# Gate projections with the tokens as the moving operand, key sums as rows, two more held input units and a fused state decay in a two-layer hybrid decoder step

## The reference

```python
def trunk(x, ...):
    for l in range(2):
        h = rmsnorm(x, gl[0])
        mix = even_mixer(h, ...) if l == 0 else odd_mixer(h, ...)
        x = x + rmsnorm(mix, gl[1])
        h = rmsnorm(x, gl[2])
        x = x + rmsnorm(squared_relu_mlp(h, w_ff1[l], w_ff2[l]), gl[3])   # 1024 -> 4096 -> 1024

def even_mixer(h, S0, ...):       # layer 0: gated DeltaNet (4 heads, 128x128 state) beside a gating MLP
    qkv, gate, beta_pre, a_pre, u_pre, v_pre = split_cols(h @ w_in, ...)  # beta_pre, a_pre: 4 columns each
    ...
    S = S * gl_c[..., None, None] + einsum('bhik,bhiv->bhkv', kd_c, v_new)

def odd_mixer(h, C0, n0, m0, ...):  # layer 1: mLSTM (4 heads, 128x256 state C, 128-element key sum n)
    q, k, v, i_pre, f_pre, o_pre = split_cols(h @ w_in, ...)              # i_pre, f_pre: 4 columns each
    ...
    Cm = keep[..., None, None] * Cm + einsum('bhj,bhjd,bhjv->bhdv', wk, k_c, v_c)
    n = keep[..., None] * n + einsum('bhj,bhjd->bhd', wk, k_c)
```

## Time and profile before

| | |
|---|---|
| median of 3 executions | 2915.94 us (2915.1 to 2921.61) |
| the profiled execution, its own time | 2918.17 us |
| span of its instructions | 2916.4 us |
| PE busy | 2785.1 us, 95% of the span |
| DVE busy, ACT busy | 1390.2 us, 1171.1 us |
| mean granted clock of TensorE | 0.961 |

### The profile page before, as it was taken

One profiled execution on the slowest core, in us unless ns is written; L12 is line 12 of the kernel. 1 busy time (PEld: TensorE's weight loads), 2 busy tenths in 40 slices (PEclk: granted clock), 3 DMA queues, 4 the chain that ended last, 5 costly groups with the idle time before them and its releaser, 6 DMA issues.

```text
span 2916.4 us, 41138 instructions
## 1 busy us (share of the span) xinstructions
PE 2785.1 (95%) x17217; PEld 2482.0 (85%) x17217; DVE 1390.2 (48%) x2130; ACT 1171.1 (40%) x2024; POOL 209.9 (7%) x343
## 2 busy tenths in 40 slices
PE   7889999799999999999999999999999899999997
PEld 5779988688888769889999998998776687999997
DVE  4545554645554446443444446434444337444344
ACT  6454445455554335333333335333332235333323
POOL 5011100100000000110000001110000000000000
PEclk9899999999999999899999999999999899999998
DMA  5343222522323224543332325543245634343222
GB/s 179 118 130 103 85 67 87 161 62 90 91 74 91 80 87 146 166 141 95 102 95 75 114 73 160 157 136 98 87 136 95 98 90 148 98 127 114 87 88 71
DMA packets 365928, 313.61 MB, mean 108 GB/s; under 512 B 11217, under 2 KB 338923, under 8 KB 365744
## 3 DMA queue, kind: packets, MB, share of 16 engines
q1 hardware_dynamic: 336224, 207.91, 25.8%
q0 software_dynamic: 29520, 103.07, 11.0%
HBM read 256.02 MB, written 54.91 MB: 107 GB/s over the span
## 4 chain that ended last, share of the span: by engine, by line
PE 73%; issue 10%; DVE 6%; ACT 6%; DMA 3%; POOL 1%; ACTq 0%; POOLq 0%; DVEq 0%
PE dense L519 60%; PE mixer L519 11%; DMA wst<-in_w_ff_dram 2%; ACT whi L993 2%; DVE wlo L1467 2%; ACT arena L993 1%; DVE hf L1610 1%; DMA xl<-xd 1%; PE mixer L735 1%; ACT ffh L993 1%; ACT L993 1%; DVE hlo L1606 0%; DVE ffh L1506 0%; ACT relu L993 0%; DVE accA L1543 0%
## 5 line engine op out<-in xcount | busy, mean ns | idle before, releaser
L519 PE MATMUL dense<-hhi,whi 128*128 128x272 f32 (+1 forms) x3072 | 865.0, 336 | 32.0 <-DVE hlo L1606 12.1
L519 PE MATMUL dense<-hhi,wlo 128*128 128x272 f32 (+1 forms) x3072 | 836.4, 327 | 0.0
L519 PE MATMUL dense<-hlo,whi 128*128 128x272 f32 (+1 forms) x3072 | 835.3, 326 | 0.0
L1467 DVE TENSOR_TENSOR wlo<-wst,whi 128x1024 fp32r<-128x1024 f32 x384 | 470.6, 1226 | 371.8 <-ACT whi L993 371.6
L519 PEld LDWEIGHTS dense<-hhi,whi 128*128 128x128 f32 x3072 | 524.4, 192 | 95.7 <-issue 32.2
L993 ACT ACTIVATE whi<-wst 128x1024 fp32r<-128x1024 f32 x384 | 404.2, 1053 | 449.8 <-PE dense L519 410.6
L519 PEld LDWEIGHTS dense<-hhi,wlo 128*128 128x128 f32 x3072 | 522.3, 192 | 43.8
L519 PEld LDWEIGHTS dense<-hlo,whi 128*128 128x128 f32 x3072 | 525.0, 192 | 38.1 <-issue 1.0
L519 PE MATMUL dense<-h1hi,whi 128*128 128x272 f32 (+1 forms) x1536 | 431.3, 335 | 18.3 <-DVE wlo L1467 11.0
L519 PE MATMUL dense<-h1lo,whi 128*128 128x272 f32 (+1 forms) x1536 | 420.8, 328 | 0.0
L519 PE MATMUL dense<-h1hi,wlo 128*128 128x272 f32 (+1 forms) x1536 | 419.1, 327 | 0.0
(11 more groups left out here) (304 smaller groups left out, 2015.8 us busy)
## 6 DMA issues: line engine op xcount, KB each, us to landing
wst<-in_w_ff_dram SPq DMA_DIRECT2D x256, 512.0 KB, 3.9
wst<-in_w_in_even_dram SPq DMA_DIRECT2D x48, 512.0 KB, 3.8
wst<-in_w_in_odd_dram SPq DMA_DIRECT2D x48, 512.0 KB, 3.8
proj<-ffh POOLq DMA_DIRECT2D x48, 272.0 KB, 2.4
proj<-ffh POOLq DMA_DIRECT2D x48, 256.0 KB, 2.3
arena<-proj POOLq DMA_DIRECT2D x8, 1536.0 KB, 9.6
wst<-in_w_out_even_dram SPq DMA_DIRECT2D x16, 512.0 KB, 3.6
xl<-xd POOLq DMA_DIRECT2D x32, 256.0 KB, 3.1
```

The source lines that it names most:

```text
L519: return pe.matmul(out, lhsT, rhs, start=start, stop=stop)
L1467: TT(wlo[:, u % 2, :], wst[:, u % 2, :], whi[:, u % 2, :].bitcast(F32), ALU.subtract)\
```

## The change

1. **Gates.** The 16 (and 8) gate columns become the stationary operand and the tokens the moving one: for each of 8 blocks of channels two products, of one matmul of 512 columns in group 0 and two of 272 in group 1. ACT copies the 16 rows into `relu2`; one dense unit later a new item `gate2` turns them to token rows and adds the two halves, with small float32 matmuls against the identity, two for each tile; DVE copies them out. The split of `wg` is an item of its own (`wgs`), four units ahead of the gate.
2. **Held units.** `SEQ_2` holds 6 units (14 and 15 added), `SEQ_1` has 18 in another order. The loads of norm 2's residual use four buffers, two of them in `relu2`.
3. **Decay.** In `gdn_sample` the multiplication and the two additions become 8 fused operations of 128x128.
4. **Key sums.** n of all samples and heads is loaded as 32 rows of 512 bytes by one DMA, turned by one PE transpose and copied into `CS` by DVE; new values are gathered by DVE, turned back at the end together with the prompt's, and stored by two DMAs. PE waits for the copies (`ms_nset`).

```diff
-SEQ_1 = [0, 20, 1, 21, 2, 22, 3, 23, 4, 5, 12, 6, 7, 13, 8, 9, 14, 10, 11, 15]
-SEQ_2 = [16, 17, 18, 19]
+SEQ_1 = [0, 20, 1, 2, 21, 3, 4, 22, 5, 6, 23, 7, 8, 12, 9, 10, 11, 13]
+SEQ_2 = [14, 15, 16, 17, 18, 19]
...
+            if gate is not None and g == 0 and i == gate - 4:
+                rows[-1].append(("wgs", l))
             if i == gate:
                 rows[-1].append(("gate", l, g))
+            if gate is not None and i == gate + 1:
+                rows[-1].append(("gate2", l, g))
...
+            if r == 0:
+                return (xl if c % 4 < 2 else relu2)[:, c % 2, :], ("xl", "xr")[c % 4 // 2] + str(c % 2), c // 4 + 1
...
             def gate(l, g):
-                for i, t in enumerate(range(*GT[g])):
-                    _, c, n = tok(t)
-                    for k in range(KT):
-                        mm(DB[0:n, b, i * 16:(i + 1) * 16], hhi[g][:, k, c], wg2[:, k, :], start=k == 0, stop=False)
-                        last = mm(DB[0:n, b, i * 16:i * 16 + 8], hlo[g][:, k, c], wg_hi[:, k, :],
-                                  start=False, stop=k == KT - 1)
+                for k in range(KT):
+                    for rows, w, x in ((16, wg2[:, k, :], hhi[g]), (8, wg_hi[:, k, :], hlo[g])):
+                        for q, (c0, c1) in enumerate(PARTS[g]):
+                            last = mm(DB[0:rows, b + q, 0:512] if g == 0 else DB[0:rows, b + q, 0:272], w,
+                                      x[:, k, 272 * q:272 * (q + 1)] if g else x[:, k, 0:512],
+                                      start=k == 0 and rows == 16, stop=k == KT - 1 and rows == 8)
+                last.then_inc(S("job_done"), 1)
+
+            def gate_turn(l, g):
+                evac_wait(pe, ("gate", l, g))
+                for i, t in enumerate(range(*GT[g])):
+                    _, c, n = tok(t)
+                    for half in range(2):
+                        last = mm(DB[0:n, b, i * 8:(i + 1) * 8], relu2[0:16, 0, c],
+                                  ident[0:16, 8 * half:8 * half + 8], start=half == 0, stop=half == 1)
...
-                    link(TT(ss, ss, bcl(gls[:, :].rearrange("p (b h) -> p b h", h=H)[:, :, h], [P, NB, P]), ALU.mult))
                     dve.wait_ge(S("gs_ds"), h + 1)
-                    for q in range(2):
-                        last = TT(ss[:, 4 * q:4 * q + 4], ss[:, 4 * q:4 * q + 4], M4(3 * q), ALU.add)
+                    for k in range(NB):
+                        last = STT(ss[:, k], ss[:, k], gls[:, k * H + h:k * H + h + 1], M4(3 * (k // 4))[:, k % 4, :],
+                                   ALU.mult, ALU.add)
...
+                    if n == NS:
+                        w("state")
+                        last = pe.transpose(MB[:, 3, 0:NB * H], m["NROW"][0:NB * H], ident[0:NB * H, 0:NB * H])
                     s(last, "kT")
...
+                    if n == NS:
+                        pe.wait_ge(S("ms_nset"), 1)
                     for h in range(H):
                         last = mm(M4(3)[:, h, 0:n], spread(h), ROWW[0:H, c])
...
+                    pe.wait_ge(S("ms_nset"), max(1, h))
...
+                    if n == NS:
+                        link(dve.tensor_copy(m["NT"].rearrange("p b h -> p (b h)"), MB[:, 3, 0:NB * H]))
+                        dve.tensor_copy(m["CS"][:, :, :, DV], m["NT"][:, :, 0:2].rearrange("p b h -> p h b"))\
+                            .then_inc(S("ms_nset"), 1)
...
+                    if half:
+                        dve.wait_ge(S("ms_upd"), (h + 1) * NB)
+                        ins = dve.tensor_copy(m["NN"][:, :, h], m["CS"][:, h % 2, :, DV])
+                        if h < 2:
+                            link(ins)
+                            ins = dve.tensor_copy(m["CS"][:, h, :, DV], m["NT"][:, :, h + 2])
+                        ins.then_inc(S("ms_nset"), 1)
...
+                elif step == "end":
+                    pe.wait_ge(S("ms_nset"), 1 + H)
+                    pe.transpose(MB[0:NB * H, 2, 0:P], m["NN"].rearrange("p b h -> p (b h)"), ident[:, :])
+                    pe.transpose(MB[0:H, 2, P:2 * P], CN[:, :, DV], ident[:, :]).then_inc(S("ms_num"), 1)
...
-                with nc.allow_non_contiguous_dma("1024 numbers"):
-                    dma(cs[:, :, DV:DV + 1], state_mlstm_n[0, :, h].rearrange("b k -> k b").unsqueeze(2))\
-                        .then_inc(S(f"ms_in{h % 2}"), 16)
...
+                    dma(ml_map(t)["NROW"][0:NB * H], state_mlstm_n[0].rearrange("b h k -> (b h) k"))\
+                        .then_inc(S("m_xin"), 16)
...
-                    with nc.allow_non_contiguous_dma("1024 numbers"):
-                        dma(n_s[0, :, h].rearrange("b k -> k b").unsqueeze(2), cs[:, :, DV:DV + 1])\
-                            .then_inc(S(f"cs_out{h % 2}"), 16)
...
+                    dma(n_s[0].rearrange("b h k -> (b h) k"), m["NROW"][0:NB * H]).then_inc(S("state_out"), 16)
+                    dma(n_p[0, 0], m["NPR"][0:H]).then_inc(S("state_out"), 16)
```

More of the change, by code:

```diff
@@ L253, in count @@
                 wide = g
[L254 removed]
+            elif item[0] in ("on", "gate", "gate2", "misc"):
                 keys, ended, reader = [item], [item], "act_evac"
[L256 removed]
+                if item == ("misc", "sgw") or item[0] == "gate2":
                     reader = "dve_evac"
[L258 removed]
+                wide = {"on": NORMS[item[1]][2] if item[0] == "on" else 0, "gate": item[-1], "gate2": 0,
+                        "misc": int(item == ("misc", "sgw"))}[item[0]]
             else:
@@ L470, in evac_wait, with xl_at @@
             eng.wait_ge(S(sem), v)
+        def xl_at(e, c):
+            r = POST.index(e)
+            if r == 0:
+                return (xl if c % 4 < 2 else relu2)[:, c % 2, :], ("xl", "xr")[c % 4 // 2] + str(c % 2), c // 4 + 1
+            if e == 15 and c < 5:
+                return xl_own[:, c, :], "xl_own", 5
+            n = c // 7 if e == 15 else c // 2
+            return xl[:, c % 2, :], f"xl{c % 2}", 4 * r - 2 + n + 1
         block = ctx.enter_context(nc.Block())
@@ L1158, in pre, with gate_weights @@
                 A_(hhi[g][:, c, :], hf2[:, c % 2, 0:GN[g]], ACT.Copy).then_inc(S("h_hi"), 1)
-            def gate(l, g):
-                if g == 0:
-                    act.wait_ge(S("wg_loaded"), 16 * (l + 1))
-                    if l:
-                        done(("gate", 0, 1))
-                    A_(wg_hi, wg[:, :, :], ACT.Copy).then_inc(S("wg_hi_ready"), 1)
+            def gate_weights(l):
+                act.wait_ge(S("wg_loaded"), 16 * (l + 1))
+                if l:
+                    done(("gate", 0, 1))
+                A_(wg_hi, wg[:, :, :], ACT.Copy).then_inc(S("wg_hi_ready"), 1)
+            def gate(l, g):
                 key = ("gate", l, g)
-                b = PLAN.jobs[key]["bank"]
-                act.wait_ge(S("cols_zero"), 1)
+                if l:
+                    act.wait_ge(S("h1_split"), FG * FK * (1 + g))
+                if g:
+                    done(("gate2", l, 0))
                 done(key)
-                t0 = GT[g][0]
-                last = A_(gates[:, t0:t0 + 4, :], DB[:, b, 0:64].rearrange("p (t c) -> p t c", c=16)[:, :, 8:16],
-                          ACT.Copy)
-                if g:
-                    last = A_(gates[0:NS, TILES, :], DB[0:NS, b, 72:80], ACT.Copy)
-                last.then_inc(S("gate_lo"), 1)
+                A_(like(relu2[0:16, 0], g), DB[0:16, PLAN.jobs[key]["bank"]:PLAN.jobs[key]["bank"] + 2, 0:272] if g
+                   else DB[0:16, PLAN.jobs[key]["bank"], 0:512], ACT.Copy).then_inc(S("act_evac"), 1)
             def softplus(name, z, v):
@@ L1582, in apply @@
                 STT(hf2[:, c % 2, 0:n], x, gain(l, q, c), rstd[:, 0:n], ALU.mult, ALU.mult).then_inc(S("n_stt"), 1)
-                if e < 15:
-                    dve.wait_ge(S(f"xl{c % 2}"), 16 * (4 * r + c // 2 + 1))
-                elif c == 0:
-                    dve.wait_ge(S("xl_own"), 16 * 5)
-                elif c >= 5:
-                    dve.wait_ge(S(f"xl{c % 2}"), 16 * (4 * r + c // 7 + 1))
-                old = xl_own[:, c, :] if e == 15 and c < 5 else xl[:, c % 2, 0:n]
+                place, name, count = xl_at(e, c)
+                dve.wait_ge(S(name), 16 * count)
+                old = place[:, 0:n]
                 dve.wait_ge(S("n_stt"), KT * e + c + 1)
@@ L2148, in norm_sum @@
                     if e < 15:
-                        xl_load(e, 0)
-                        xl_load(e, 1)
+                        for c in range(4 if e == POST[0] else 2):
+                            xl_load(e, c)
                 else:
@@ L2297, in _ @@
                 elif item[0] == "ap":
-                    if item[1] < 15 and item[2] < KT - 2:
-                        xl_load(item[1], item[2] + 2)
+                    ahead = 4 if item[1] == POST[0] else 2
+                    if item[1] < 15 and item[2] < KT - ahead:
+                        xl_load(item[1], item[2] + ahead)
                     if item == ("ap", 15, 5):
```

115 lines of the change are left out of this document (70 added, 45 removed).

## The result

| | before | after |
|---|---|---|
| median | 2915.52 us (4 executions, 2912.60 to 2921.61) | 2837.14 us (4 executions, 2834.32 to 2845.64) |
| profiled execution, its own time | 2918.17 us | 2834.74 us |
| mean granted clock | 0.961 | 0.981 |

The ratio is 0.9729, 95% interval 0.9703 to 0.9755: 79 us faster, where 57 were forecast. The direction was right, the amount was not.

The account below looks back on a forecast made before the run. PE, busy 95% of the span, was taken to bound the kernel. Gates 34, held units 6, decay 0 and key sums 17 summed to 57 us, giving a median of 2859 us; range 2838 to 2884, 8 times in 10.

Parts of the forecast that it names:

- Gate matmuls and clock: Four gates: matmuls and turns 24.0 us for 48.1, 24 saved; 7 us more from clock no longer lost behind them.
- the first rival: Narrow gates run at the low clock: 28 us less gain, 2887 us; chance 12%.
- Gate waits: At the gates: 5.40 us wait for wg's split goes, 2.5 us given back.
- 1.5 for `wlo`: Behind the gate: DVE is late next, the wait for wlo can return; 1.5 us given back.
- 1 for a pair of banks: Group 1 gates: next unit gets the pair read last and waits for a slow convolution eviction; 1 us back.
- Held units: Two group 1 units moved from the DeltaNet stretch to norm 2: net 6 us saved, between -4 and 11.
- the 3 that I gave it: Thinned DeltaNet stretch: 8 more places where PE steps meet without a piece between; 3 us cost, bounds 0 and 13.
- The third rival: Thinned stretch gives held units' gain back: 8 places at 3.68 us, 29 us instead of 3, 2885 us; chance 6%.
- Decay: Samples' state update: eight fused operations add 0.9 us a head while PE runs dense pieces; counted 0, -2 to 1.
- Key sums: Samples' part: without single-number DMAs, weight-load waits and low clock behind them go; net 17 us, between 8 and 20.
- The rival by which the weights wait for C and not for n: Samples' weight loads are held by C's 1 MB transfers, so the 17 us do not come: 2876 us; chance 12%.
- the slower one: PE's five new waits for n's copies, at 19.37 us each, cost 97 us against 57: 2956 us; chance 2%.

Follow-up runs that it names:

- the form alone: Difference of two runs on the kernel before: gates' part alone (2860.73 us) against bank skipped with early split, old-form gate matmuls (2884.92 us); 25 us.
- the early split: Kernel before, one bank skipped behind each group 0 gate and wg split four units ahead, old-form gate matmuls: 2884.92 us, ratio 0.9900.
- the bank: Kernel before with one bank of the rotation skipped behind each group 0 gate, nothing else: 2903.05 us, ratio 0.9955.
- samples' waits: Changed kernel with samples' masked values made an item earlier, inside existing items: 2810.01 us, 25 us below the changed kernel on the same chip.

## Why the prediction was off, step by step

**Gate matmuls and clock: right mechanism, size a little high.** 24 + 7 = 31 us forecast, 25 measured as the form alone, with an interval that reaches 31. The 24 were counted from 13.65 us for a group 0 gate, which holds 2.4 us that belong to the wait in front of it, and from 12.53 for the other, which takes 11.0 without its wait. The 3.7 and 4.0 us of the new gates are exact, and the first rival (low clock for narrow operands) did not come.

**Gate waits: this step failed.** I wrote "5.4 - 2.5" for it, 2.9 us: the wait for `wg`, less 1.5 for `wlo` and 1 for a pair of banks. The runs show 29 us in its place, 16 for the early split and 13 for the bank. I missed that the wait itself had already cost the gate its clock; that a second wait for `wg`, 1.24 us, stands at layer 1's gate; and that one more job in the rotation changes which read-outs the units behind it wait for, up to the next job that takes a pair of banks. There I had even the sign wrong: I looked at the turn's own neighbours in group 1, and not at the jobs of group 0 behind it. The wait for `wlo` that I expected back did come, at 1.34 us.

**Held units.** Forecast 6, measured 5 with overlapping intervals, which is not enough to call it right. In the trace the waits at norm 2 fell from 6.94, 2.11 and 2.84 to 1.19, 0.77 and 3.22 us, 6.7 less. But with the old order and the four buffers they are 5.28, 2.11 and 3.20, so 1.3 of the 6.7 belong to the buffers and 5.4 to the order. From 171.43 to 576.49 us, which takes in the stretch and the norm, PE idles only 2.2 us less than with the old order over the same 2604 matmuls, so some 3 us came back as small gaps, which is the 3 that I gave it. The net of the order is nearer 2 us than 6. The third rival, 3.68 us a place, did not come.

**Decay.** 0 forecast, nothing that can be told from nothing measured.

**Key sums.** 17 forecast, 17 measured (11 to 22). PE's waits of 6.13 and 8.15 us became 2.37 and none, in the kernel with this part alone too, and the three loads of the earlier trace rows have left its chain. The rival by which the weights wait for C and not for n would have given nothing: it is refuted by the kernel with this part alone. So is the slower one, since PE waits at no head for the copies of n.

The forecast said that it would fail "mostly by the clock". It failed by waits that I had not looked for, plain rows of PE at 159 and 1232 us, in the stretches just behind the work that the change touches.

## What to carry to other kernels

Where buffers rotate by counting, one job more or less moves the waits behind it, until something realigns the count: list, for each job of the new order, whose read-out it waits for, and compare with the old list before pricing anything. Price a wait of the matrix engine at more than its length: 6.6 us of waits were worth 16 here, 5.8 us 13, and 14 us of samples' waits 25, each to within 5 to 8 us. And make what the matrix engine reads one item earlier than it reads it, without adding items to a list that is spread by its length.

## What the hardware showed that I had not expected

**The same code loses the clock in some executions and not in others.** The changed kernel, profiled twice, over the same 1460 matmuls between two gaps:

```profile
1824.90:2086.12 261.22, 254.08 (x1460) 221.85 (x1459) 119.55 (x199) 95.75 (x186) 14.00 (x19) 0.99 0.40 116
```

```profile
1817.02:2086.23 269.21, 261.96 (x1459) 228.09 (x1459) 119.52 (x199) 95.78 (x186) 13.96 (x19) 0.96 0.39 112
```

8 us apart, all of it PE's, at 0.99 and 0.96. The 6.6 us without a gate in them, seen above, lie in this part of the program and are of this size. I take them to be of this kind, since no part of the change is needed for it; shown it is not. Over its ten executions the kernel took from 2829.93 us at a mean clock of 0.982 to 2848.29 at 0.976; the kernel with the decay in three operations took 2828.97 at 0.984 and 2845.89 at 0.976. Time follows the clock on one line, about 3 us for a thousandth, and kernels whose real difference is nothing lie on the same line. For small differences it is worth comparing the time times the clock, which over those ten executions stays between 2777 and 2783 us (the clock is given to a thousandth, itself 3 us): 2780 us for the changed kernel, 2780 with the decay in three operations, 2801 before. By this measure 21 of the 79 us are work and waits, and the rest is clock. With the old order of units it is 2778, so it shows nothing for the held units either.

**Moving columns can be nearly free.** 96 instead of 16 beside a load of 128 stationary columns cost nothing at the first gate (13.7 us either way) and 1.6 us over all four.
